# Moving a causal convolution from TensorE transposes to accumulating DMAs

## The reference

```
proj = rms_norm(x) @ w_in                     # z | xBC | dt | q | k | v | g_ssm | g_att
xbc  = silu(causal_depthwise_conv(xbc, conv_w, conv_b))     # 4 taps: u[t], u[t-1], u[t-2], u[t-3]
xs, Bm, Cm = split(xbc, [4096, 4096 + 1024])
y    = ssd_chunked(xs, dt, A, Bm, Cm)         # decay = exp(a[l] - a[s]) below the diagonal; uses xs * dt
y    = y + d_skip * xs
y    = rms_norm_per_group(y * silu(z)) * norm_w
```

## Time and profile before

| | |
|---|---|
| Median of 3 runs (lowest, highest) | 2054.71 us (2053.49, 2055.02) |
| Profiled execution, its own time | 2054.78 us |
| its span, first to last instruction | 2053.2 us |
| PE busy | 2043.5 us, 100% |
| DVE busy | 1564.7 us, 76% |
| ACT busy | 1171.4 us, 57% |
| POOL busy | 171.0 us, 8% |
| Granted TensorE clock, mean | 1.000 |

### The profile page before, as it was taken

The page is one execution under the profiler, slowest core; times in us unless marked ns, Lnnn a source line. Parts: engine busy times, 40 slices in busy tenths (PEclk is TensorE's granted clock), DMA queues, the critical chain, the costliest instruction groups (busy, mean ns, idle before and its releaser), DMA issues.

```text
span 2053.2 us, 28102 instructions
## 1 busy us (share of the span) xinstructions
PE 2043.5 (100%) x9594; PEld 1678.5 (82%) x9594; DVE 1564.7 (76%) x1860; ACT 1171.4 (57%) x1496; POOL 171.0 (8%) x195
## 2 busy tenths in 40 slices
PE   9999999999999999999999999999999999999999
PEld 8888877778888888888888888888888888887777
DVE  6777866665866777777667887888898889878866
ACT  5444555554556666666655454556666666655543
POOL 1121000000011222222000000010000000000000
PEclk9999999999999999999999999999999999999999
DMA  7656675654566666666565657598888888666574
GB/s 250 198 182 204 188 221 166 174 165 144 184 203 187 186 184 185 187 190 184 168 192 188 210 165 236 186 305 248 255 246 245 254 257 252 189 209 220 181 238 155
DMA packets 220626, 419.80 MB, mean 204 GB/s; under 512 B 16449, under 2 KB 22002, under 8 KB 220290
## 3 DMA queue, kind: packets, MB, share of 16 engines
q1 hardware_dynamic: 212162, 399.48, 62.0%
q0 software_dynamic: 7776, 18.94, 4.4%
q10 hardware_dynamic: 608, 0.34, 0.1%
HBM read 410.25 MB, written 4.26 MB: 202 GB/s over the span
## 4 chain that ended last, share of the span: by engine, by line
PE 91%; DVE 4%; DMA 3%; ACT 1%; issue 0%; SPq 0%; DVEq 0%; ACTq 0%
PE acc L2244 72%; PE side L2331 8%; PE acc L2331 6%; PE side L2260 3%; DMA w_raw<-in_w_ffn_down 2%; DVE w_lo L2036 2%; PE side L2400 1%; PE side L2547 1%; ACT w_hi L1216 1%; DVE w_raw L1951 1%; DMA x_row<-in_x 0%; DMA w_raw<-in_w_in 0%; PE acc L2260 0%; PE side L2560 0%; DVE w_lo L1257 0%
## 5 line engine op out<-in xcount | busy, mean ns | idle before, releaser
L1257 DVE TENSOR_TENSOR w_lo<-w_raw,w_hi 128x1024 fp32r<-128x1024 f32 x332 | 419.5, 1276 | 248.6 <-ACT w_hi L724 247.5
L724 ACT ACTIVATE w_hi<-w_raw 128x1024 fp32r<-128x1024 f32 x332 | 348.4, 1057 | 357.3 <-PE acc L2244 318.1
L2244 PE MATMUL acc<-w_hi,h_hi 128*128 128x512 f32 x1248 | 498.5, 399 | 0.1
L2244 PE MATMUL acc<-w_hi,h_lo 128*128 128x512 f32 x1248 | 487.0, 390 | 0.0
L2244 PE MATMUL acc<-w_lo,h_hi 128*128 128x512 f32 x1248 | 485.9, 389 | 0.0
L2244 PEld LDWEIGHTS acc<-w_hi,h_hi 128*128 128x128 f32 x1248 | 234.4, 188 | 52.2 <-issue 6.9
L2244 PEld LDWEIGHTS acc<-w_hi,h_lo 128*128 128x128 f32 x1248 | 234.2, 188 | 50.3
L2244 PEld LDWEIGHTS acc<-w_lo,h_hi 128*128 128x128 f32 x1248 | 234.7, 188 | 47.8 <-issue 1.9
L1930 DVE TENSOR_TENSOR w_lo<-w_raw,w_hi 128x1024 fp32r<-128x1024 f32 x136 | 165.2, 1221 | 38.0 <-ACT w_hi L1137 35.5
L1053 ACT ACTIVATE w_hi<-w_raw 128x1024 fp32r<-128x1024 f32 x110 | 116.5, 1060 | 117.3 <-PE acc L2244 72.7
L1137 ACT ACTIVATE w_hi<-w_raw 128x1024 fp32r<-128x1024 f32 x136 | 143.1, 1058 | 66.1 <-PE acc L2244 50.4
(11 more groups left out here) (437 smaller groups left out, 3450.2 us busy)
## 6 DMA issues: line engine op xcount, KB each, us to landing
w_raw<-in_w_in SPq DMA_DIRECT2D x320, 512.0 KB, 4.3
w_raw<-in_w_ffn_down SPq DMA_DIRECT2D x88, 512.0 KB, 4.9
w_raw<-in_w_ffn_gate SPq DMA_DIRECT2D x68, 512.0 KB, 4.5
w_raw<-in_w_ffn_up SPq DMA_DIRECT2D x68, 512.0 KB, 5.3
w_raw<-in_w_ssm_proj SPq DMA_DIRECT2D x64, 512.0 KB, 4.6
side_raw<-in_w_ffn_up SPq DMA_DIRECT2D x40, 512.0 KB, 4.8
w_raw<-in_w_attn_proj SPq DMA_DIRECT2D x32, 512.0 KB, 3.7
w_raw<-in_w_out SPq DMA_DIRECT2D x32, 512.0 KB, 5.0
```

The costliest lines, as they stand in the source:

```text
L724: nc.scalar.activation(w_hi[:, r], w_raw[:, n % RING], ACT.Copy).then_inc(hi_ready, 1)
L1257: nc.vector.tensor_tensor(w_lo[:, r], w_raw[:, n % RING], w_hi[:, r].bitcast(F32), ALU.subtract).then_inc(lo_ready, 1)
L2244: done = nc.tensor.matmul(acc[p][:, t], a[:, k0 + kk, cut], w[:, r, kk], start=first and kk == n == 0, stop=last and kk == UK - 1 and n == ...
```

## The change

The convolution stays with tokens in partitions. DVE multiplies `x_proj` by three taps, each broadcast over the partitions (`conv_products`, after z0), then by its own tap, and adds the bias (`conv_own`, after z1). A shift by tokens is then a shift by partitions, and POOL issues accumulating DMAs from SBUF to SBUF for it (`shifted`): the product for three tokens back onto the one for two, by one row; the product for one token back onto `x_proj`, by one row; then the sum onto `x_proj`, by two rows. Each is a DMA over 127 or 126 partitions and a small one for the rows that pass from the first token half to the second. The taps and the bias are loaded for each group by POOL, as broadcasts (`taps_load`). The 16 transposes `x_T` and `xs_T` of a group are gone, and with them ACT's first tap and its copy to `y_row`.

The rest moves: `exps` to after z6 and z7, SiLU (`conv_silu`) to after the next x0, `decays` to after z7 and the next x0, `xdt` (`x_scaled`) to after the next x1, `y_products` from x1 to x3, `y_rows` from x3 to x5, `tail_gated` to x5, `tail_squares` to x6, `tail_normed` from x6 to after z1 of the next z chunk (behind `conv_own`), and `y_columns` from z0 to z2. `one_back`, `three_back` and `conv_bias_b` lie where `decay` lies, so `exps` waits for the first shifts too (`shift_one`).

```diff
-        conv_x = at("conv_x", 191, [P, CT, T])
+        late_taps = at("late_taps", 191, [P, TT, CW])
+        one_back = at("one_back", 167, [P, TT, CW])
+        three_back = at("three_back", 171, [P, TT, CW])
+        taps_b = at("taps_b", 138, [P, TAPS, CW])
+        conv_bias_b = at("conv_bias_b", 175, [P, 1, CW])
...
+            def conv_silu(g):
+
+                act.wait_ge(shift_two, g * 32 + 32)
+                nc.scalar.activation(x_proj[:], x_proj[:], ACT.Silu).then_inc(xs_ready, 1)
...
-                    if u == 1 and not head:
+                    if u == 0 and not head:
+                        conv_silu(g - 1)
+                    if u == 3 and not head:
...
+                if not head:
+
+                    act.wait_ge(xdt_ready, g)
+                    act.wait_ge(skip_ready, g)
                 for t in range(TT):
                     last = nc.scalar.activation(x_proj[:, t], acc[0][:, t], ACT.Copy, scale=x_rstd[:, t:t + 1])
                 last.then_inc(x_rows_ready, 1)
+                act.wait_ge(x_rows_ready, g + 1)
+                nc.scalar.sem_inc(acc_free[0], 1)
...
+                if hf == 0:
+
+                    act.wait_ge(shift_one, g * 64 + 64)
...
-                    if u == 0:
-
-                        act.wait_ge(x_T, g + 1)
-                        for n in range(CT):
-                            last = conv_first_taps(sums(0)[:, n], g * CT, conv_x[:, n], n)
-                        last.then_inc(conv_first, 1)
                     if u == 1:
                         act.wait_ge(cb_sum, g + 1)
                         nc.scalar.activation(cb[:], side[:, 0, 0:3 * P], ACT.Copy).then_inc(cb_ready, 1)
-                    if u == 2:
-                        act.wait_ge(conv_done, g + 1)
-                        nc.scalar.activation(conv_x[:], conv_x[:], ACT.Silu).then_inc(xs_ready, 1)
-                        exps(g, 0, head)
-                    if u == 3:
-                        exps(g, 1, head)
-                    if u == 5:
-
-                        act.wait_ge(xdt_ready, g + 1)
-                        nc.scalar.activation(y_row[:], side[:, 2:4], ACT.Copy).then_inc(xrow_ready, 1)
+                    if u in (6, 7):
+                        exps(g, u - 6, head)
...
+            def conv_products(g):
+
+                dve.wait_ge(x_rows_ready, g + 1)
+                dve.wait_ge(taps_in, g * 32 + 32)
+                for out, back in ((one_back, 1), (three_back, 3), (late_taps, 2)):
+                    last = nc.vector.tensor_tensor(out[:], x_proj[:], taps_b[:, TAPS - 1 - back].unsqueeze(1).broadcast_to([P, TT, CW]),
+                                                   ALU.mult)
+                link(last)
+
+            def conv_own(g):
+                link(nc.vector.tensor_tensor(x_proj[:], x_proj[:], taps_b[:, TAPS - 1].unsqueeze(1).broadcast_to([P, TT, CW]), ALU.mult))
+                nc.vector.tensor_tensor(x_proj[:], x_proj[:], conv_bias_b[:].broadcast_to([P, TT, CW]), ALU.add).then_inc(conv_ready, 1)
...
+            def tail_step(g, u):
+                if u == 0:
+                    decays(g, 1)
+                if u == 1:
+                    x_scaled(g)
+                if u == 5:
+                    tail_gated(g)
+
+            def x_chunk(g, head):
+                for u in range(UPC):
+                    split_lo()
+                    if not head:
+                        tail_step(g - 1, u)
+
             def z_chunk(g, head):
-                by_head = "p (h d) -> p h d"
                 for u in range(UPC):
                     split_lo()
                     if u == 0:
-                        dve.wait_ge(conv_first, g + 1)
-                        for back in range(1, TAPS):
-                            conv_taps(g, back)
-                    if u == 1 and not head:
+                        conv_products(g)
+                    if u == 1:
+                        conv_own(g)
+                        if not head:
+                            tail_normed(g - 1)
+                    if u == 3 and not head:
                         tail_transposed(g - 1)
-                    if u == 2:
...
+            def shifted(target, source, back, landed):
+
+                pool.dma_start(target[back:P], source[0:P - back], accum_op=ALU.add).then_inc(landed, 16)
+                pool.dma_start(target[0:back, 1], source[P - back:P, 0], accum_op=ALU.add).then_inc(landed, 16)
+
+            def conv_group(g):
+
+                mask = mask_sl.unsqueeze(1).broadcast_to([P, HG // 2, P])
+                for hf, (ready, count) in enumerate(((conv_ready, g + 1), (shift_one, g * 64 + 64))):
+                    blocks = acs_b[:, hf].rearrange("p h (t l) -> p h t l", l=P)
                     pool.wait_ge(acs_in[hf], g * 16 + 16)
-                    blocks = acs_b[:, hf].rearrange("p h (t l) -> p h t l", l=P)
-                    nc.gpsimd.tensor_tensor(blocks, blocks, mask, ALU.add).then_inc(acs_masked, 1)
+                    nc.gpsimd.tensor_tensor(blocks[:, :, 0], blocks[:, :, 0], mask, ALU.add)
+                    pool.wait_ge(ready, count)
+                    nc.gpsimd.tensor_tensor(blocks[:, :, 1], blocks[:, :, 1], mask, ALU.add).then_inc(acs_masked, 1)
+                    if hf == 0:
+                        shifted(late_taps, three_back, 1, shift_one)
+                        shifted(x_proj, one_back, 1, shift_one)
+                    else:
+                        shifted(x_proj, late_taps, 2, shift_two)
...
+            def next_group(i, first=False):
 
                 pool.wait_ge(decay_exp, i * 2 + 2)
                 loads(i + 1)
+                taps_load(i + 1)
+                skip(i, first)
                 tail(i)
-                group(i + 1)
+                conv_group(i + 1)
...
             def tail_between(g):
                 def between(u):
-                    if u == 1:
+                    if u == 3:
                         y_products(g)
-                    if u == 3:
+                    if u == 5:
                         y_rows(g)
                 return between
 
             def y_columns(g):
                 pe.wait_ge(y_ready, g + 1)
-
-                pe.wait_ge(xrow_ready, g + 1)
                 to_columns(y_row, 0).then_inc(y_T, 1)
 
             def z_between(g, first=False):
                 def between(u):
                     if u == 0:
-
-                        pe.wait_ge(x_rows_ready, g + 1)
-                        for n in range(CT):
-                            for t in range(TT):
-                                at_col = (n % 2) * T + t * P
-                                last = transpose(acc[0][:, n // 2, at_col:at_col + P], x_proj[:, t, n * P:(n + 1) * P])
-                        last.then_inc(x_T, 1)
                         pe.wait_ge(bT_ready, g + 1)
                         if first:
                             pe.wait_ge(acs_ready, 2)
@@ -2593,17 +2626,11 @@
                         c_late = bc[:, bass.ds(g + G, 1), P:T].rearrange("p o t -> p (o t)")
                         nc.tensor.matmul(side[:, 0, 0:T], bT[:, 0:P], c_rows, start=True, stop=True)
                         nc.tensor.matmul(side[:, 0, T:T + P], bT[:, P:T], c_late, start=True, stop=True).then_inc(cb_sum, 1)
-                        if not first:
-                            y_columns(g - 1)
-                    if u == 4:
-
-                        pe.wait_ge(xs_ready, g + 1)
-                        if not first:
-                            pe.wait_ge(yT_ready, g)
-                        for n in range(CT):
-                            for t in range(TT):
-                                last = transpose(side[:, 2 + t, n * P:(n + 1) * P], conv_x[:, n, t * P:(t + 1) * P])
-                        last.then_inc(xs_T, 1)
+                    if u == 2 and not first:
+                        y_columns(g - 1)
+                    if u == 6 and not first:
+
+                        pe.wait_ge(yT_ready, g)
```

More of the change, by code:

```diff
@@ L2203, in _ @@
             pool.dma_start(acs_dram[:], acsT[:]).then_inc(acs_out, 16)
+            taps_load(0)
             pool.wait_ge(acs_out, 16)
             loads(0)
-            group(0)
-            with repeat(pool, G - 1, [(own, 2)]) as i:
+            conv_group(0)
+            def next_group(i, first=False):
                 pool.wait_ge(decay_exp, i * 2 + 2)
                 loads(i + 1)
+                taps_load(i + 1)
+                skip(i, first)
                 tail(i)
-                group(i + 1)
+                conv_group(i + 1)
+            next_group(0, True)
+            with repeat(pool, G - 2, [(own, 2)]) as i:
+                next_group(i + 1)
+            skip(G - 1)
             tail(G - 1)
@@ L2615, in last_columns @@
             def last_columns(u):
[L2616 removed]
+                if u == 2:
                     y_columns(G - 1)
```

93 lines of the change are left out of this document (39 added, 54 removed).

## The result

| | before | after |
|---|---|---|
| Median (lowest, highest) | 2054.10 us (2052.28, 2055.02), 4 runs | 2163.03 us (2162.55, 2166.13), 4 runs |
| Ratio, 95% interval | | 1.0531 [1.0518, 1.0543] |
| Profiled execution's span | 2053.2 us | 2161.5 us |
| PE busy | 2043.5 us, 9594 instructions | 2068.2 us, 9466 instructions |
| Granted TensorE clock, mean | 1.000 | 0.975 |

The change costs 109 us. The forecast was 2121, with a range to 2155: the sign was right, the time 42 us too low and outside the range.

The account below looks back on a forecast made before the run. PE was taken to bound the kernel, busy 2043.5 of 2053.2 us. The terms -13.9 + 37.1 + 0.7 + 37.6 + 4.9 = +66.4, on a median of 2054.71, gave 2121 us (chance 0.62), with a range of 2098 to 2155.

Parts of the forecast that it names:

- The transposes removed, -13.9: Two blocks of eight transposes leave PE's list, 1.74 us a group, 13.9 us less in 8 groups.
- PE's busy time would be 14 less: A sign to look for in the profile after: PE's busy time lower by 14 us.
- The wait at `y_columns`: After z2, PE waits for `y_row` behind DVE's queue: 5.3 us in groups 1 to 7, 37.1, plus 0.7 in the last.
- E + 14.1: Forecast end of DVE's scaling of `y_row`, 14.1 us after E, the end of x7 on PE.
- The wait at `y_products`: After x3, PE waits for `xdt` from DVE: 4.7 us in each of 8 groups, 37.6 us.
- The shifts: First large shifts land by E + 25.8, covered by the first wait except in group 0: 4.9 us more at `y_products`.
- One engine for 127 partitions: Rival: a large shift goes through one DMA engine, 35 us in each of 8 groups, 2400 us; chance 0.10.
- the first rival: PE's clock drops in the new waits, 15 waits x 1.9 = 28 us, 2149 us; chance 0.13.
- The weights, "I give them nothing": Shifts, taps and bias add 9 + 4 us of all DMA engines a group beside the weight loads; counted as zero.
- the fourth rival: `y_row` and `xdt` are ready before PE asks, so only the 13.9 us saving remains: 2041 us; chance 0.06.
- the forecast's 0.58: Time in us taken for POOL's issue of each large shift, from a load with 4 KB rows.

Follow-up runs that it names:

- filled: The changed kernel with 22 spare products of the constant `ones` on PE in front of `y_columns` and of `y_products`: 2129.92 us.
- spread: The changed kernel with the same work in another hand-written order, meant to have each of PE's inputs made before PE asks: 2127.83 us.
- loads_no_shifts: spread_loads without the six accumulating transfers of a group, so x is not convolved: 2040.67 us.
- normed_first: The changed kernel with DVE's scaling of `y_row` put ahead of the convolution's products: 2160.33 us.
- products_x4: The changed kernel with `y_products` after x4 instead of x3 on PE: 2129.21 us.
- before_traffic: The kernel before with the change's transfers alone (taps, bias, three accumulating transfers a group) into spare room: 2085.33 us.
- spread_loads: spread with each group's taps, bias and `acs_b` loads drawn apart and PE's wait for `yT` in z7 dropped: 2078.75 us.

## Why the prediction was wrong

- *The transposes removed, -13.9*: right (12, from 9.7 to 15.2). But "PE's busy time would be 14 less" was wrong: it is 24.7 more.
- *The wait at `y_columns`*: right, place, cause and size: 5.3 forecast, 5.36 in the group shown, E + 14.1 both times.
- *The wait at `y_products`*: right in place and cause, 5.3 instead of 4.7. POOL's two instructions of `skip` (849.63, 3.02 us for both) lay beside two of DVE's, the decay product (2.08 us instead of 1.22) and the split before `xdt` (2.06): some 1.7 us, where I took 1.0. Over 8 groups it is 43.1 us instead of 37.6.
- *The shifts*: right, in group 0 too (4.5 us, forecast 4.9), but PE stood there at the weights, whose split ACT has queued behind the shifts, and `y_products` waited 6.3 us in addition, 1.0 more than in the other groups. The second large one was forecast to land at E + 25.8 and POOL was released at 834.07, E + 26.3; ACT came to it at 837.22. One engine for 127 partitions: false, the first large shift of a group landed in 7.5 to 8.0 us, the second, issued beside it, in 10.3 to 11.0, where the forecast had 8.0 and 11.0. The Trainium skill, "DMA: Bandwidth & Descriptors", in the section on why a DMA increments its semaphore by 16, names an exception by which some direct copies issued from GpSimd use all 16 engines. These landings agree with the exception and not with the rule that would put 127 rows on one.
- *The step that failed* is the dismissal of the first rival, that "the clock falls in the waits". I gave it 0.13 because "the column of the granted clock reads 1.00 there and everywhere". But the kernel before has no stretch in which PE idles for 5 us inside the program, so that column could not show what an idle time does: the absence of a case was read as evidence against it. The one row that did bear on it, 236 ns for the first products and 118 for the later ones, spoke for a slow start after rest, although the column read 1.00 there too (1.20 to 5.00). The warning in the Trainium skill, "TensorE: Matmul & The Clock Gate", in its table of what matters for kernels, that an idle gap brings the clock down, stood beside it, and these traces agree: behind each of the 15 waits of 5.0 to 6.3 us the clock was 0.50. Its size was low too: 15 x 1.9 = 28, measured 38.6 by PE's busy time, for 16 falls, and 33 by filled. With the rival's 28 the sum was 2149; the waits, 85.7 instead of 80.3, and the larger price of a fall are the rest of the 42 us.
- *The weights, "I give them nothing"*: right for this kernel (ACT's wait for `w_raw` 29.2 us against 32.7). The reason that the runs point to is not in the prediction: PE's own waits gave the ring time to fill. In the covered order (spread) the time is 87 us over the 2041 of the fourth rival, which left this limit out; loads_no_shifts shows that 2041 is right for PE's list.

## What to carry to other kernels

A wait that is added on TensorE is priced twice, once for its length and once for the slower clock behind it; if it can't be removed, fill it with products, or put the consumer a unit later. Shorter waits are no safe ground: some of 2.0 to 2.4 us were followed by a fall (below). A clean granted clock before a change proves nothing about gaps that weren't there yet. When bytes are added beside a stream of weights, multiply DMA share by the loop's length before and after, and ask separately whether each burst fits in what the ring holds ahead.

## What the hardware showed

- Behind waits of 5.3 us the granted clock was 0.50 for up to 4.7 us (`y_columns`) and 5.8 us (`y_products`), costing 2.2 and 2.8 us. Behind the waits at the weights in normed_first, 3.1 to 4.8 us, it fell as well (0.52 from 840.29 to 843.30).
- Behind waits of 2.1 to 2.2 us it was 1.00 in all 8 places of products_x4. Elsewhere it fell behind waits of such lengths: in before_traffic behind 4 of 7 waits for `y_row` of 2.3 to 2.4 us, in spread_loads behind two of the waits for `w_lo` of 2.0 us. One of these, with its windows:

```profile
872.13 0.50 PE L2300 MATMUL acc<-w_hi,h_hi 128*128 128x512 f32 x1 [2.01 <-DVE w_lo L1266]
```

```profile
872.13:873.40 1.27, 1.27 (x6) 1.05 (x6) 0.48 (x1) 1.27 (x4) 0.00 (x0) 1.00 1.42 239
873.40:876.50 3.10, 3.10 (x9) 2.41 (x8) 3.02 (x3) 3.07 (x4) 0.78 (x1) 0.50 0.81 207
```

- The large accumulating SBUF to SBUF transfers of the kernel after, 508 and 504 KB over 127 and 126 partitions, landed in 7.5 to 8.0 us (first of a group), 10.3 to 11.0 (second, issued 1.2 us behind it) and 5.6 to 7.2 (third, alone). By the difference between spread_loads and loads_no_shifts, three of them and their small ones took some 10 us of all 16 DMA engines a group.
- The issue of such a transfer on POOL shows as 0.8 to 1.7 us, but successive ones start 0.5 to 0.6 apart (821.56, 822.19, 822.73, 823.27 in the kernel after), so the forecast's 0.58 held.
